# Issuing the window-cache copies of samples 0 to 3 during the output projection instead of the input projections

## The chip, the cores and the metric

The kernel runs on one core of one Trainium2 chip. The metric is device time in microseconds (us) of one execution. Times are given as the median of several executions; the profile shows one execution.

## The reference

One inference step of a one-layer decoder, for a prompt of 512 tokens and for 8 samples of 8 new tokens each (64 rows). Model width is 1024, all in 32-bit floats. Cut to what matters here:

```python
mod = (silu(c) @ w_ada + b_ada)                     # shift, scale and gate, 6 x 1024 per sequence
proj = (x * (1 + scale1) + shift1) @ w_in           # 1024 -> 3072: q, k, v of mixers A and B
oa, (wk, wv) = attend_a(qa, ka, va)                 # dilated window attention, 8 heads x 64
ob = rms_norm(attend_b(qb, kb, vb, lam), subln_g)   # differential attention, 4 heads
mixed = concatenate([oa, ob]) @ w_o
x = layer_norm(ALPHA * x + gate1 * mixed)
u = (x * (1 + scale2) + shift2) @ w_up + b_up       # 1024 -> 5632
uc = causal_conv3(u, w_conv) + b_conv
y = (gelu(uc[:half]) * uc[half:]) @ w_down + b_down
x = layer_norm(ALPHA * x + gate2 * y)

# for the samples, mixer A also returns its window buffers, moved on by the 8 new rows:
kk = concatenate([cache_win_k, k], 1)               # (8, 2048 + 8, 8, 64)
vv = concatenate([cache_win_v, v], 1)
return o, (kk[:, 8:], vv[:, 8:])                    # outputs win_k_sample, win_v_sample
```

The last line is what the change is about: of each sample's key window and value window, 2040 old rows of 2 KB each go unchanged from an input array to an output array. That is 4,080 KB (4.18 million bytes) per array and sample, 16 such copies in all.

## The kernel before, in words

Five engines run their own instruction lists and meet at semaphores: PE (matmul), DVE, ACT, POOL and SP. SP computes nothing; it waits and issues nearly all DMAs, on one queue (q1). ACT issues a part of the value-cache loads on a second one (q10).

The stages, in order of time in the profiled execution:

1. Up to about 58 us: constants, the conditioning vector, the first `w_ada` chunks, x transposed and modulated.
2. About 58 to 250 us: the input projection, six sections `s` of 512 columns, each for five row tiles `t` (four of the prompt, and `TP` = 4, the samples). Each section needs one 2 MB chunk of `w_in`. After a section, SP loads the next free chunk.
3. About 250 to 310 us: the prompt's attention A, with the other `w_ada` chunks loading; about 310 to 655 us: the samples' attention over their caches, with the prompt's attention B between.
4. About 690 to 756 us: the output projection, over the row tiles `WO_TILES = [0, 1, TP, 2, 3]`. DVE adds the residual and normalises each tile (L1355 is the last instruction of a tile and raises `x1_ok`). SP then stores the tile to the scratch array `spill` (L623), because `x_sb` is overwritten by the next stage: ACT's casts into `x_sb_r` (L806) wait for `spilled`.
5. About 771 to 1058 us: the up projection, 44 steps `k` of 128 columns. A `w_up` chunk (two DMAs of 1 MB, L470) holds four steps. Steps 0 to 3 read chunk up0, 4 to 7 up1, 8 to 11 up2, 12 to 15 up3, and so on. There are two buffers for raw chunks, so the load of up(i+2) is issued when PE has finished up(i) (`w_used`).
6. The down projection, the last norm, the stores.

Every weight is split into a high part and a rest before PE can use it. In the up projection, DVE makes the high part of a quarter of the chunk after next use (`high_of_piece(12 + k)`, a CAST at L1037) at the head of its step `k`, ahead of that step's convolution (L1411 to L1418); POOL then makes the rest (L741) at the head of its own step `k`. PE's step 4i waits for a quarter's rest before each quarter of its products (`wl_rest`). So the four quarters of up2 are made in steps 4 to 7 of DVE and POOL and are read from step 8 on.

The copies between input and output are made by one helper, which touches no engine but the DMA engines:

```python
def move_window(i, names=(("cache_win_k", "wks"), ("cache_win_v", "wvs"))):
    for name, dst in names:
        sp.dma_start(o[dst][0, i, 0:PAST - DS], a[name][0, i, DS:PAST]).then_inc(copied, 16)
```

`copied` is waited for only at the very end. Before the change, both copies of sample 0 are issued ahead of the projection sections, those of samples 1 to 3 after sections 0 to 2; the eight copies of samples 4 to 7 are issued one at a time behind the loads of up2 to up9.

Of the kernel before, what the change touches and what calls it, by code (L numbers as in the profile page):

```python
# [52 lines left out]
def chunk_before(n):  # L53

    return max((i for i in range(n) if SLOT_OF[i] == SLOT_OF[n]), default=None)
# [19 lines left out]
def build(nc, a, o, spill):  # L75
# [6 lines left out]
    with ctx:  # L82
# [3 lines left out]
        def sem(name):  # L86
            return ctx.enter_context(nc.semaphore(name))
# [40 lines left out]
        def slot(i, t=ring):  # L128
            return t[:, i * SLOT:(i + 1) * SLOT].rearrange("p (k n) -> p k n", k=KT_D)
# [120 lines left out]
        ada_ok = sem("ada_ready")  # L250
# [203 lines left out]
        def _(sp):  # L454
            def load_chunk(n):
                kind, i = CHUNKS[n]
                if (prev := chunk_before(n)) is not None and CHUNKS[prev][0] == "down":
                    half, kg = divmod(CHUNKS[prev][1], 3)
                    sp.wait_ge(g_used, FT * half + min(FT, 8 * kg + 8))
                elif prev is not None:  # L460
                    sp.wait_ge(w_used, prev + 1)
                if CHUNKS[n] == ("ada", 6):
                    sp.wait_ge(w_used, CHUNK_AT[("in", 5)] + 1)
                s = w_in_slot[SLOT_OF[n]]
                dst = slot(SLOT_OF[n])
                src = a[{"ada": "w_ada", "in": "w_in", "o": "w_o", "up": "w_up", "down": "w_down"}[kind]][0]
                src = src.rearrange("(k p) n -> p k n", p=P)
                if kind == "up":
                    for g in range(2):
                        sp.dma_start(dst[:, :, 256 * g:256 * g + 256],  # L470
                                     src[:, :, DFF * g + 256 * i:DFF * g + 256 * i + 256]).then_inc(s, 16)
                elif kind == "down":
                    half, kg = divmod(i, 3)
                    nk = min(8, FT - 8 * kg)
                    sp.dma_start(dst[:, 0:nk, :], src[:, 8 * kg:8 * kg + nk, CH * half:CH * half + CH]).then_inc(s, 16)
                else:
                    sp.dma_start(dst, src[:, :, CH * i:CH * i + CH]).then_inc(s, 16)
# [32 lines left out]
# [5 lines that stand above are left out]
            def flat(ap):  # L515
                return ap.rearrange("t h d -> t (h d)")

            sp.wait_ge(ada_ok, 4)
            move_window(0)
            n_rope = n_v = 0  # L520
            for n, (s, t) in enumerate(units):
                kb_rows = slice(P * t, P * t + P)
                if s in (0, 3):
                    n_rope += 1
                elif s in (1, 4):
                    m = s // 3
                    sp.wait_ge(rope_ok, n_rope + 1)
                    if t < TP:
                        st = n_rope % 4
                        dst = flat((o["wkp"] if m == 0 else o["kkp"])[0, 0])[kb_rows, :]  # L530
                        sp.dma_start(dst, stage[:, st, :]).then_inc(stg[st], 16)
                    else:
                        if m == 0:
                            for b in range(DB):
                                sp.dma_start(flat(o["wks"][0, b])[PAST - DS:PAST, :],
                                             k_s[DS * b:DS * b + DS, 0, :]).then_inc(out_sem, 16)
                        else:
                            sp.dma_start(o["kks"][0].rearrange("b s h d -> (b s) (h d)"), k_s[:, 1, :]).then_inc(out_sem, 16)
                    n_rope += 1
                else:  # L540
                    m = s // 3
                    n_v += 1
                    sp.wait_ge(pj_a, n_v)
                    if t < TP:
                        dst = flat((o["wvp"] if m == 0 else o["kvp"])[0, 0])[kb_rows, :]
                        sp.dma_start(dst, vp[:, t, m, :]).then_inc(out_sem, 16)
                    elif m == 0:
                        for b in range(DB):
                            sp.dma_start(flat(o["wvs"][0, b])[PAST - DS:PAST, :],
                                         v_s[DS * b:DS * b + DS, 0, :]).then_inc(out_sem, 16)  # L550
                    else:
                        sp.dma_start(o["kvs"][0].rearrange("b s h d -> (b s) (h d)"), v_s[:, 1, :]).then_inc(out_sem, 16)
                if t == TP:
                    load_chunk(6 + s)
                    if s < 3:
                        move_window(s + 1)
            for n in range(12, 18):
                load_chunk(n)

# [55 lines left out]
                sp.dma_start(ln1[:, i, :], a[name].to_broadcast([P, D])).then_inc(ln_in, 16)  # L615
            sp.dma_start(st_r, a["state_conv"][0].rearrange("b j f -> (b j) f")).then_inc(st_in, 16)

            for i, t in enumerate(WO_TILES):
                if i == TP:
                    load_chunk(FIRST_LATE + 2)  # L620
                sp.wait_ge(x1_ok, i + 1)
                rows = P if t < TP else NS
                sp.dma_start(spill[P * t:P * t + rows, :], x_sb[0:rows, t, :]).then_inc(spilled if i < TP else spilled_last, 16)  # L623
            load_chunk(FIRST_LATE + 3)
            sp.wait_ge(st_mm, 11)
            for i, name in enumerate(("b_down", "ln2_g", "ln2_b")):
                sp.dma_start(ln2[:, i, :], a[name].to_broadcast([P, D])).then_inc(ln2_in, 16)
# [38 lines left out]
        def _(pool):  # L666
# [21 lines left out]
            for _, what, r in sorted(jobs):  # L688
                if what == "split":
                    n = CHUNK_AT[("in", r)]  # L690
                    for k in range(0, KT_D, 2):
                        if r == 0:
                            pool.wait_ge(in0_high, k // 2 + 1)
                        else:
                            pool.wait_ge(win_high, 4 * (r - 1) + k // 2 + 1)
                        w = slot(SLOT_OF[n])[:, k, :]
                        high, rest = pair_of(n, k)
                        nc.gpsimd.tensor_tensor(rest, w, high.bitcast(F32), ALU.subtract).then_inc(win_pool, 1)
                    if r == 0:
                        rest_of_ht(0)  # L700
                    continue
                s, t = units[rope_units[r]]
                sample_k = s in (1, 4) and t == TP
                pool.wait_ge(pj_d, r + 1)
                if not sample_k and r >= 4:
                    if (prev := last_t[r]) is not None:
                        pool.wait_ge(qk_t, prev)
                    if (q := last_store[r]) > 0:
                        pool.wait_ge(stg[r % 4], 16 * q)
                rows = P if t < TP else NS  # L710
                dst = k_s[:, s // 3, :] if sample_k else stage[0:rows, r % 4, :]
                nc.gpsimd.tensor_tensor(dst, tmp_a[0:rows, r % 2, :], tmp_b[0:rows, r % 2, :], ALU.add)\
                    .then_inc(rope_ok, 1)
# [56 lines left out]
        def _(act):  # L770
# [47 lines left out]
            for _, what, n in sorted(jobs):  # L818
                s, t = units[n]
                rows = P if t < TP else NS  # L820
                if what == "v":
                    act.wait_ge(pj_mm, n + 1)
                    dst = vp[:, t, s // 3, :] if t < TP else v_s[:, s // 3, :]
                    nc.scalar.activation(dst, bk(n % 4)[0:rows, :], ACT.Copy).then_inc(pj_a, 1)
                else:
                    k = tr_units.index(n)
                    act.wait_ge(qk_t, k + 1)
                    src = bk(4 + k % 2).rearrange("p (f t) -> p f t", f=4)
                    m0 = 8 * (s // 3)
                    for h in range(2):  # L830
                        last = nc.scalar.activation(qtp[64 * h:64 * h + 64, m0 + h:m0 + 8:2, P * t:P * t + P],
                                                    src[64 * h:64 * h + 64], ACT.Copy)
                    last.then_inc(qk_a, 1)
# [1208 lines left out]
```

## Time and profile before

| | |
|---|---|
| median of 3 runs | 1250.76 us (1249.6 to 1254.75) |
| the profiled execution | 1249.29 us, of which the span from first to last instruction is 1247.3 us |
| mean granted PE clock | 0.911 of full speed |
| busy: PE, DVE, POOL, ACT | 1059.1, 838.5, 356.9, 269.2 us |
| queue q1 (SP) | 250.82 MB, 59.2% of 16 DMA engines' span |
| queue q10 (ACT) | 24.19 MB, 5.7% |
| the window copies | 16 of 4,080 KB |

The profile has a timeline of instructions for each engine. For a DMA it gives the time at which it was issued and how long the issuing engine was held, and separately the time from issue to landing, when its semaphore is raised. Busy shares are averages over stages with different limits; what one stage costs has to be read from its own windows.

### The profile page before, as it was taken

What the parts mean: (1) busy time and instruction counts of PE and PEld (TensorE: products, weight loads), DVE (VectorE), ACT (ScalarE), POOL (GpSimd) and SP (SyncE); (2) the same over time, 40 slices, a digit from 0 to 9 for tenths busy, and PEclk for the clock granted to TensorE, in tenths of its full rate; (3) what the DMA queues carried; (4) which work ended last, traced back from release to release, by engine and by line L of the source; (5) the groups of instructions that cost most, each with busy time, mean ns of one, the idle gap of its engine ahead of it and who ended that gap; (6) DMA issues with size and microseconds to landing.
All of it is one profiled execution on the core that took longest, in us unless ns stands there. A gap on an engine that the chain in (4) does not pass through costs nothing.

```text
span 1247.3 us, 24201 instructions
## 1 busy us (share of the span) xinstructions
PE 1059.1 (85%) x9389; PEld 856.2 (69%) x9389; DVE 838.5 (67%) x1521; ACT 269.2 (22%) x588; POOL 356.9 (29%) x378
## 2 busy tenths in 40 slices
PE   4599999999677677777776996999999999999994
PEld 2377777666455455555545774999999999777772
DVE  1657457267665767667749568367677676998968
ACT  0310010232222223222234103223222232100002
POOL 2333243100000000000007004356565565434323
PEclk8699999999787788779787897999999999999997
DMA  8948894686999999999991206177557731412202
GB/s 305 404 163 314 306 363 148 215 298 231 315 296 307 336 352 303 342 326 320 317 316 60 63 26 219 62 275 270 203 202 254 283 137 69 147 56 89 75 27 76
DMA packets 112551, 276.55 MB, mean 222 GB/s; under 512 B 9608, under 2 KB 33174, under 8 KB 108837
## 3 DMA queue, kind: packets, MB, share of 16 engines
q1 hardware_dynamic: 99125, 250.82, 59.2%
q10 hardware_dynamic: 13312, 24.19, 5.7%
q8 instruction: 75, 1.23, 0.4%
q14 instruction: 39, 0.32, 0.1%
HBM read 264.60 MB, written 76.69 MB: 274 GB/s over the span
## 4 chain that ended last, share of the span: by engine, by line
PE 58%; DVE 17%; SPq 10%; DMA 7%; issue 5%; POOL 2%; ACT 1%; ACTq 0%; DVEq 0%; POOLq 0%; PEldq 0%
PE wide L1572 16%; PE wide L1573 15%; PE wide L1574 15%; DVE ring L1145 3%; DMA ring<-in_cache_k 3%; SPq L591 3%; PE wide L1646 2%; SPq L593 2%; DMA ring<-in_w_ada 2%; PE wide L1635 2%; DVE ring_r L1077 2%; PE wide L1521 1%; SPq L448 1%; DMA ring<-in_w_down 1%; PE wide L1697 1%
## 5 line engine op out<-in xcount | busy, mean ns | idle before, releaser
L741 POOL TENSOR_TENSOR ring_r<-ring,ring_r 128x1024 fp32r<-128x1024 f32 x70 | 184.4, 2642 | 273.5 <-DVE ring_r L1037 204.5
L1572 PE MATMUL wide<-x_sb_r,ring_r 128*128 128x288 f32 x704 | 211.6, 301 | 8.2 <-DVE ht_r L1059 5.1
L1573 PE MATMUL wide<-ht_r,ring_r 128*128 128x288 f32 x704 | 209.4, 298 | 0.0
L1574 PE MATMUL wide<-x_sb_r,ring_r 128*128 128x288 f32 x704 | 208.6, 296 | 0.0
L1574 PE MATMUL wide<-ring_r,ht_r 128*128 128x512 f32 (+1 forms) x400 | 158.7, 397 | 0.0
L1145 DVE STREAM_TRANSPOSE ring<-ring 128x512 f32<-128x512 f32 x208 | 129.2, 674 | 34.7 <-DMA ring<-in_cache_k 34.7
L1572 PEld LDWEIGHTS wide<-x_sb_r,ring_r 128*128 128x128 f32 x704 | 133.4, 190 | 11.7 <-issue 11.2
L1574 PEld LDWEIGHTS wide<-x_sb_r,ring_r 128*128 128x128 f32 x704 | 134.2, 191 | 0.0
L1573 PEld LDWEIGHTS wide<-ht_r,ring_r 128*128 128x128 f32 x704 | 133.8, 190 | 0.0
L1697 PE MATMUL wide<-ring,x_sb 128*32 128x128 f32 (+1 forms) x1792 | 70.9, 309 | 49.5 <-DVE ring L1145 47.9
L1572 PE MATMUL wide<-ring_r,x_sb_r 128*128 128x512 f32 (+1 forms) x240 | 97.7, 407 | 11.0 <-DVE ht_r L1059 8.9
L1697 PEld LDWEIGHTS wide<-ring,x_sb 128*32 128x32 f32 x1792 | 54.5, 127 | 66.9 <-DVE ring L1145 57.5
L723 POOL COPY x_sb<-ring 32x128 f32<-32x128 f32 x64 | 18.4, 287 | 272.9 <-PE wide L1697 270.8
L1573 PE MATMUL wide<-ring_r,x_sb_r 128*128 128x512 f32 (+1 forms) x240 | 95.1, 396 | 0.0
L1572 PE MATMUL wide<-ring_r,ht_r 128*128 128x512 f32 (+1 forms) x220 | 88.2, 401 | 4.3 <-DVE ht_r L1397 2.4
L1574 PEld LDWEIGHTS wide<-ring_r,ht_r 128*128 128x128 f32 (+1 forms) x400 | 72.6, 181 | 21.5
L1573 PE MATMUL wide<-ring_r,ht_r 128*128 128x512 f32 (+1 forms) x220 | 86.7, 394 | 0.0
L1411 DVE SCALAR_TENSOR_TENSOR room<-room,vec_t 128x512 f32<-128x512 f32 x44 | 59.9, 1361 | 39.7 <-ACT room L954 39.6
L946 ACT ACTIVATE room<-wide,vec_t 128x576 f32<-128x576 f32 x44 | 32.7, 744 | 206.2 <-PE wide L1574 201.5
L1413 DVE SCALAR_TENSOR_TENSOR room<-room,vec_t 128x512 f32<-128x512 f32 x44 | 69.5, 1579 | 1.6
L1646 PE MATMUL wide<-room 128*128 128x128 f32 x320 | 58.3, 320 | 11.0 <-ACT room L866 9.8
L1037 DVE CAST ring_r<-ring 128x1024 fp32r<-128x1024 f32 x62 | 41.9, 687 | 36.1 <-DMA ring<-in_w_up 29.7
(225 smaller groups left out, 1894.0 us busy)
## 6 DMA issues: line engine op xcount, KB each, us to landing
ring<-in_cache_k SPq DMA_DIRECT2D x128, 256.0 KB
out_wks<-in_cache_win_k SPq DMA_DIRECT2D x8, 4080.0 KB, 19.0
out_wvs<-in_cache_win_v SPq DMA_DIRECT2D x8, 4080.0 KB, 24.7
ring<-in_w_ada SPq DMA_DIRECT2D x12, 2048.0 KB, 10.2
ring<-in_w_up SPq DMA_DIRECT2D x22, 1024.0 KB, 7.3
ring<-in_cache_win_k SPq DMA_DIRECT2D x16, 1024.0 KB
ring<-in_w_in SPq DMA_DIRECT2D x6, 2048.0 KB, 18.5
room<-in_cache_v ACTq DMA_DIRECT2D x32, 256.0 KB
```

The costliest lines, as they stand in the source:

```text
L591: pg = sp.value_load(pages[0:1, N_PAGES * b + 4 * g + t:N_PAGES * b + 4 * g + t + 1], min_val=0, max_val=a["cache_k"].shape[1] - 1)
L741: nc.gpsimd.tensor_tensor(rest, w, high.bitcast(F32), ALU.subtract).then_inc(wl_rest, 1)
L946: nc.scalar.activation(u_b[:, k % 2, 2:2 + NT].rearrange("p (h t) -> p h t", h=2), pair, ACT.Identity, bias=vec_t[:, 0, 48 + f:49 + f]).th ...
L1037: nc.vector.tensor_copy(pair_of(n, slice(k, k + 2))[0], slot(SLOT_OF[n])[:, k:k + 2, :]).then_inc(wl_high, 1)
L1145: last = nc.vector.transpose(ktg[:, G % NK, :, 32 * t:32 * t + 32], kraw[G % NK][:, t, :].rearrange("p (g d) -> p g d", d=32))
L1411: then(nc.vector.scalar_tensor_tensor(out=c_p, in0=u_b[:, k % 2, 1:1 + SEQ], scalar=tap(1), in1=c_p, op0=ALU.mult, op1=ALU.add))
L1413: nc.vector.scalar_tensor_tensor(out=c_p, in0=u_b[:, k % 2, 0:SEQ], scalar=tap(0), in1=c_p, op0=ALU.mult, op1=ALU.add)
L1572: nc.tensor.matmul(out, left[0], right[0], start=first, stop=False)
L1573: nc.tensor.matmul(out, left[0], right[1], start=False, stop=False)
L1574: return nc.tensor.matmul(out, left[1], right[0], start=False, stop=last)
L1646: last = nc.tensor.matmul(bank[:, 0:P], pt_b[:, u % 2, P * kb:P * kb + P], vp[:, kb, m, P * (n // 2):P * (n // 2) + P], start=(kb == 0), s ...
L1697: last = nc.tensor.matmul(bank[32 * nn:32 * nn + 32, at:at + nk], qbd[:, w % 2, g].rearrange("p i q -> p (i q)"), keys[:, g, 0:nk], start= ...
```

## The change

The four calls of `move_window` for samples 0 to 3 leave the projection stage. Samples 0 and 1 (four copies) are issued right after the loads that precede the output projection's tiles, samples 2 and 3 (four copies) right behind the load of chunk up1 (`FIRST_LATE + 3`). A wait of SP on `ada_ok` that stood ahead of the first call goes as well.

```diff
-            sp.wait_ge(ada_ok, 4)
-            move_window(0)
             n_rope = n_v = 0
             for n, (s, t) in enumerate(units):
...
                 if t == TP:
                     load_chunk(6 + s)
-                    if s < 3:
-                        move_window(s + 1)
             for n in range(12, 18):
                 load_chunk(n)
...
             sp.dma_start(st_r, a["state_conv"][0].rearrange("b j f -> (b j) f")).then_inc(st_in, 16)
 
+            move_window(0)
+            move_window(1)
             for i, t in enumerate(WO_TILES):
                 if i == TP:
                     load_chunk(FIRST_LATE + 2)
...
             load_chunk(FIRST_LATE + 3)
+            move_window(2)
+            move_window(3)
             sp.wait_ge(st_mm, 11)
```

Only SP's list changes. From the load of the gains and of the convolution state ahead of the output projection (`st_r`) to the load of up2, SP issues this before the change (each row is a DMA, destination and source, shape; L623 stores the tiles, the two L470 rows load up0 and up1):

```order
L616 DMA room<-in_state_conv 16x5632
L623 DMA x_spill<-x_sb 128x1024 x2
L623 DMA x_spill<-x_sb 64x1024
L623 DMA x_spill<-x_sb 128x1024
L470 DMA ring<-in_w_up 128x8x256 x2
L623 DMA x_spill<-x_sb 128x1024
L470 DMA ring<-in_w_up 128x8x256 x2
L627 DMA room<-in_b_down 128x1024
L627 DMA room<-in_ln_g 128x1024
L627 DMA room<-in_ln_b 128x1024
L470 DMA ring<-in_w_up 128x8x256 x2
```

In the changed kernel, the same stretch of SP's list, up to the load of the last gain row:

```order
L612 DMA room<-in_state_conv 16x5632
L512 DMA out_wks<-in_cache_win_k 64x16320
L512 DMA out_wvs<-in_cache_win_v 64x16320
L512 DMA out_wks<-in_cache_win_k 64x16320
L512 DMA out_wvs<-in_cache_win_v 64x16320
L621 DMA x_spill<-x_sb 128x1024 x2
L621 DMA x_spill<-x_sb 64x1024
L621 DMA x_spill<-x_sb 128x1024
L470 DMA ring<-in_w_up 128x8x256 x2
L621 DMA x_spill<-x_sb 128x1024
L470 DMA ring<-in_w_up 128x8x256 x2
```

```order
L512 DMA out_wks<-in_cache_win_k 64x16320
L512 DMA out_wvs<-in_cache_win_v 64x16320
L512 DMA out_wks<-in_cache_win_k 64x16320
L512 DMA out_wvs<-in_cache_win_v 64x16320
L627 DMA room<-in_b_down 128x1024
L627 DMA room<-in_ln_g 128x1024
L627 DMA room<-in_ln_b 128x1024
```

Four copies now stand ahead of the tile stores and the load of up0, and four more stand behind the load of up1, ahead of three row loads and the load of up2.

## Rows read from the trace of the kernel before

**Rows 1.** The page: busy time of each engine, its share, instructions
```profile
PE 1059.1 (85%) x9389; PEld 856.2 (69%) x9389; DVE 838.5 (67%) x1521; ACT 269.2 (22%) x588; POOL 356.9 (29%) x378
```

**Rows 2.** Stages: window, length; busy by engine; PE clock, DMA share, GB/s
```profile
58.00:250.00 192.00, 187.03 (x857) 141.06 (x858) 104.79 (x193) 19.80 (x40) 57.23 (x49) 0.99 0.74 256
704.00:750.00 46.00, 45.85 (x226) 33.61 (x225) 30.22 (x52) 0.81 (x4) 0.00 (x0) 1.00 0.09 29
780.00:803.00 23.00, 23.00 (x165) 23.00 (x165) 8.55 (x16) 6.80 (x8) 9.72 (x16) 0.94 0.00 1
```

**Rows 3.** Waits of PE, 58 to 250 us, the longest one
```profile
PE wide L1623 <- PE wide L1574: 1.8, 4, 0.5
```

**Rows 4.** Timeline of SP in the projections: issue time, SP held for
```profile
47.33 0.59 SPq L512 DMA_DIRECT2D out_wks<-in_cache_win_k  x1
47.97 0.94 SPq L512 DMA_DIRECT2D out_wvs<-in_cache_win_v  x1
...
151.19 0.41 SPq L477 DMA_DIRECT2D ring<-in_w_in  x1
151.64 10.88 SPq L512 DMA_DIRECT2D out_wks<-in_cache_win_k  x1
```

**Rows 5.** Landing of L512's copies issued from 40 to 60 us
```profile
DMA to landing us min/median/max: 18.3/24.1/29.8
```

**Rows 6.** Landing of L477's load issued at 151.19 us
```profile
DMA to landing us min/median/max: 19.8/19.8/19.8
```

**Rows 7.** Timeline of SP, output and up projection
```profile
693.73 0.43 SPq L616 DMA_DIRECT2D room<-in_state_conv  x1
714.28 36.76 SPq L623 DMA_DIRECT2D x_spill<-x_sb  x4
751.09 1.52 SPq L470 DMA_DIRECT2D ring<-in_w_up  x2
...
766.15 1.49 SPq L470 DMA_DIRECT2D ring<-in_w_up  x2
...
803.87 1.01 SPq L470 DMA_DIRECT2D ring<-in_w_up  x2
804.92 1.20 SPq L512 DMA_DIRECT2D out_wks<-in_cache_win_k  x1
830.00 1.00 SPq L470 DMA_DIRECT2D ring<-in_w_up  x2
```

**Rows 8.** Landing of L616's load, issued at 693.73 us
```profile
DMA to landing us min/median/max: 8.3/8.3/8.3
```

**Rows 9.** Landing of L470's two halves of up0, issued from 751.09 us
```profile
DMA to landing us min/median/max: 6.2/7.4/8.6
```

**Rows 10.** The same for up1: second half issued at 766.6 us
```profile
L470 SPq DMA_DIRECT2D ring<-in_w_up x2: 435/724/1012, 766.1 to 766.6; - x2
DMA to landing us min/median/max: 6.2/7.5/8.7
```

**Rows 11.** The same for up2: second half issued at 804.3 us
```profile
DMA to landing us min/median/max: 5.5/6.7/8.0
```

**Rows 12.** Landing of L512's copy issued at 804.92 us
```profile
DMA to landing us min/median/max: 18.7/18.7/18.7
```

**Rows 13.** Timeline of DVE: start, length, line, [idle before it, releaser]
```profile
762.37 3.37 DVE L1355 TENSOR_TENSOR x_sb<-x_sb,room 128x1024 f32<-128x1024 f32 x1
...
839.61 0.69 DVE L1037 CAST ring_r<-ring 128x1024 fp32r<-128x1024 f32 x1 [4.06 <-DMA ring<-in_w_up]
```

**Rows 14.** Timeline of POOL: rest of up3's last quarter
```profile
856.92 2.40 POOL L741 TENSOR_TENSOR ring_r<-ring,ring_r 128x1024 fp32r<-128x1024 f32 x1 [1.39 <-DVE ring_r L1037]
```

**Rows 15.** Timeline of ACT: first modulation of the second stage
```profile
766.52 2.78 ACT L791 ACTIVATE ht<-wide,mod_t 128x512 f32<-128x512 f32 x4 [2.40 <-PE wide L1546]
```

**Rows 16.** Stages around the start of the up projection, columns as above
```profile
770.00:776.70 6.70, 3.83 (x12) 2.94 (x12) 6.70 (x6) 3.97 (x8) 6.28 (x4) 0.50 1.07 373
776.70:782.60 5.90, 5.87 (x23) 5.68 (x24) 2.77 (x3) 0.00 (x0) 3.53 (x3) 0.50 0.29 112
```

## Prediction

> **What bounds the kernel now.** I read the page first, then the busy time by stages, the waits of PE in the stage that loses the copies, and last SP's timeline with the landing times of its transfers in the stages that receive them. PE is busy 1059.1 us, 85% of the span [rows 1], but that is an average; what counts is the two ends of the move.
>
> At the end that is relieved, PE is busy 187.03 of the 192 us from 58 to 250 us, at a clock of 0.99, with the DMA engines at 0.74 of their time [rows 2]. The longest group of waits of PE there is 1.8 us, on PE itself [rows 3], and none of the groups names a DMA. So this stage is bound by PE and the copies are already hidden in it. At the receiving end the DMA engines are nearly idle for a while: 0.09 of 704 to 750 us, and 0.00 of 780 to 803 us [rows 2]. The question is whether the moved transfers fit into these two holes, because what is issued behind them on SP's queue has to land on time.
>
> **How the queue behaves.** Two copies issued at 47.33 and 47.97 us [rows 4] landed after 18.3 and 29.8 us [rows 5], at 65.6 and 77.8 us. They are served one after the other, 12.1 us each, which is 4.18 MB at 345 GB/s. A load issued behind a copy waits for it: the one at 151.19 us took 19.8 us [rows 6], where up2's second half, on an empty queue, took 8.0 us [rows 11]. And the queue is full at some point: SP was held for 10.88 us on the copy issued at 151.64 us [rows 4], when one earlier copy and the load were outstanding. So a third copy in a row will probably hold SP until the first has landed. That does not change the order or the rate, since the DMA engines keep work throughout.
>
> **What is removed.** Eight copies, 8 x 12.1 = 97 us of DMA time, out of the projections. No wait of PE hangs on them, so I take 0. The upper bound of a gain is all of PE's idle time in that stage, 192 - 187.03 = 5.0 us. The wait on `ada_ok` had nothing behind it but these copies and much later stores: 0.
>
> **What is added ahead of the tile stores (samples 0 and 1).** The load ahead of them lands at 693.73 + 8.3 = 702.0 us [rows 7, 8]. Four copies take 4 x 12.1 = 48.4 us and end at 750.4 us. Queued behind are the stores of tiles, the first of them ready at 714.28 us [rows 7]: three of 1.31 MB together, at 345 GB/s 3.8 us, to 754.2 us; the fourth (0.52 MB, issued just before 751.09 us) to 755.7 us; then up0, 2.10 MB, 6.1 us more, to 761.8 us. It landed at 751.6 + 8.6 = 760.2 us before [rows 7, 9], so it is 1.6 us late. ACT casts it, and ACT's next instruction behind those casts started at 766.52 us after 2.40 us of idleness that PE ended [rows 15]. That idleness covers the 1.6 us: 0. If the copies went at 13 us each, up0 would be 5.2 us late and some 3 us of it would reach PE; this is the upper bound. Below nothing, POOL's work on up0 would start later and no longer overlap the DVE instruction at 762.37 us, which took 3.37 us there [rows 13] and for which PE waits; I allow 2 us of gain. The stores themselves are needed by ACT's casts from 769 us on, well behind 755.7 us.
>
> **What is added behind up1 (samples 2 and 3).** This is the term that decides.
> - up1 lands at 766.6 + 8.7 = 775.3 us [rows 10]. Four copies: + 48.4 = 823.7 us. The hole from 780 to 803 us takes only about half of them.
> - Behind them come three row loads of 0.52 MB and up2 of 2.10 MB, together 3.67 MB. At the 373 GB/s that loads reached from 770 to 776.7 us [rows 16] that is 9.8 us. up2 is there at 833.5 us; before, its second half landed at 804.3 + 8.0 = 812.3 us [rows 11].
> - From landing to use: in up3, where DVE and POOL did the same four steps with almost no wait for PE, the first cast started at 839.61 us on the load's landing [rows 13] and the last quarter's rest was ready at 856.92 + 2.40 = 859.3 us [rows 14], so 19.7 us. For up2 the last quarter would be ready at 833.5 + 19.7 = 853.2 us.
> - PE uses it at three quarters of step 8. Steps take (830.00 - 803.87) / 4 = 6.5 us [rows 7], step 8 begins at 830.0 us, so the need is at 834.9 us. PE stops for 853.2 - 834.9 = 18.3 us, in four pieces within step 8. Put otherwise: up2 could land as late as 815.2 us without harm, 2.9 us later than before, and it lands 21 us later.
> - The clock: after a stretch with PE half idle (3.83 of 6.70 us busy), it was granted 0.50 and kept that for another 5.9 us of continuous work [rows 16]. The same after this stall costs 0.5 x 5.9 = 3.0 us. Bounds 0 and 4 us.
> - Later chunks: up3 is issued at 830.0 us as before, lands behind sample 4's copy (12.1 us) at about 851 us, and DVE comes to it only after step 7, at about 855 us. PE's step 12 has moved by 21 us as well, and up4 is issued 21 us later into an idle queue. So the delay is paid once. The other direction: were up3 more than about 4 us later still, each us would be added.
>
> Queued behind SP's held issues are only DMAs of this same list, and nobody but PE, through DVE and POOL, waits for them at that time.
>
> **The rate.** For a copy alone I have 12.1 us from the pair; the copy issued at 804.92 us landed after 18.7 us [rows 7, 12], 11.3 us after up2 (812.3 us). With 11.3 us each up2 would land 3.2 us earlier, so the stall would be 15 us. I take 12.1 us, since it is the one taken between two copies in a row, which is what happens here.
>
> The Trainium skill says in "DMA: Bandwidth & Descriptors", section "Anatomy of one DMA", that a transfer costs some 2.0 us plus its bytes at 436 GB/s (a fit for DMAs issued by GpSimd). By it a copy in a row would take 9.6 us, the four 38.4 us, the stall would be 8.3 us, and the estimate of the whole change +11 us instead of +21. The trace disagrees for this kind of copy, which reads and writes main memory: 12.1 us.
>
> **Sum.** 0 + 0 + 18.3 + 3.0 = +21.3 us. The profiled execution took 1249.3 us, so 1270.6 us. It lies 1.5 us under the median of the runs, so I predict a median of 1271 to 1272 us, say 1271.5.
>
> **The rivals.**
> 1. *The first four copies bite too* (12 in 100). If they take 13 us each, or if SP, held on the third and fourth copy, is late with the stores, the stage at 770 us starts 3 to 5 us late on top. For it: the margin is only about 2 us. Against: ACT's idleness [rows 15], and a queue that should be empty of copies at 750 us. Time: 1275 to 1278 us.
> 2. *Half the stall* (10 in 100). Copies are faster when fewer other transfers run, or DVE and POOL catch up faster than 19.7 us. A rate near that of loads, 373 GB/s, gives 11.2 us for each copy and a stall of 14.7 us; a catch-up at DVE's bare busy time would take a few us more off. Time: 1258 to 1266 us. The skill's rule above is at this end too.
> 3. *The copies are not in the way* (6 in 100). If later loads overtook earlier copies on the queue, up2 would be on time and nothing else changes: 1250 us. The 19.8 us against 8.0 us speak against it.
> 4. *Faster* (4 in 100). One mechanism: without copies beside them the projections lose their idle time, 5.0 us, and some of the matmuls' own slack. It decides only if up2 lands by 815.2 us, which needs rival 3's overtaking too, or copies of under 7.5 us each. For it: DMA share of 0.74 in that stage. Against: no wait there names a DMA. Time: 1243 to 1246 us.
>
> **How the numbers follow.** The forecast (68 in 100) spans its own bounds: stall 15 to 20, clock 0 to 4, early gain 0 to 5, output projection -2 to +3, mostly not all at one end: +14 to +25 us, 1264 to 1275 us on the median. With rival 1 above and the upper part of rival 2 below, 1260 to 1278 us holds about 8 in 10. What a measurement of this kernel can tell from no change is about 0.5%, 6.3 us: faster 0.04, same 0.06, slower 0.90.
>
> **What would show it.** In the changed kernel's profile: (a) PE's busy time and clock from 58 to 250 us as before, and every stage up to 690 us at the same time within 2 us; (b) DMA share near 1 from 702 to 750 us and from 775 to 833 us; (c) SP held for about 12 us on the third and the fourth copy of each group; (d) up2's landing 27 to 30 us after its issue, and DVE's first wait at L1037 for `in_w_up` grown from 4 to about 25 us; (e) PE waiting at L1572 for POOL's L741 at step 8, some 18 us in all, with the clock at 0.50 in and after it; (f) steps of 6.5 us again from step 9 on. The prediction is wrong if PE's stage up to 250 us gets shorter by more than 2 us, or if a second chunk is late.

## The result, and the profile after

The changed kernel takes 1270.4 us (median of 4 runs, 1267.25 to 1271.24) against 1250.18 us before (median of 4, 1245.33 to 1254.75). The ratio is 1.0156, with a 95% interval of 1.0133 to 1.0179: slower by 20 us. The forecast was 1271.5 us.

The page after: the span and the busy times.

```profile
span 1265.3 us, 24201 instructions
PE 1060.6 (84%) x9389; PEld 857.1 (68%) x9389; DVE 833.2 (66%) x1521; ACT 269.7 (21%) x588; POOL 352.6 (28%) x378
```

The span is 18.0 us longer. PE is busy only 1.5 us longer than in [rows 1]; the other 16.5 us are idleness of PE. The windows of the changed kernel (columns as in [rows 2]) say where:

```profile
58.00:250.00 192.00, 187.11 (x874) 140.59 (x877) 106.46 (x200) 20.35 (x41) 57.30 (x49) 1.00 0.29 101
702.00:750.00 48.00, 47.85 (x236) 35.29 (x235) 30.55 (x52) 0.81 (x4) 0.00 (x0) 1.00 0.97 330
775.00:833.00 58.00, 52.78 (x372) 52.37 (x372) 14.38 (x26) 12.23 (x15) 12.69 (x21) 0.94 0.99 334
830.00:860.00 30.00, 15.45 (x78) 14.59 (x79) 23.40 (x26) 6.08 (x8) 18.63 (x25) 0.77 1.00 368
```

The projections lost 60% of their DMA work (0.74 to 0.29) and PE is as busy there as before: 187.11 against 187.03 us. The output projection now has the DMA engines full, 0.97 against 0.09, and PE does not notice. Of these windows, the one in which PE is half idle is that from 830 us on. SP's timeline there (issue time, SP held for):

```profile
713.94 36.77 SPq L621 DMA_DIRECT2D x_spill<-x_sb  x4
750.75 1.73 SPq L470 DMA_DIRECT2D ring<-in_w_up  x2
...
763.66 1.52 SPq L470 DMA_DIRECT2D ring<-in_w_up  x2
765.22 1.61 SPq L512 DMA_DIRECT2D out_wks<-in_cache_win_k  x1
...
768.14 0.59 SPq L512 DMA_DIRECT2D out_wvs<-in_cache_win_v  x1
...
803.42 20.12 SPq L470 DMA_DIRECT2D ring<-in_w_up  x2
823.58 3.49 SPq L512 DMA_DIRECT2D out_wks<-in_cache_win_k  x1
829.55 0.99 SPq L470 DMA_DIRECT2D ring<-in_w_up  x2
...
875.50 0.99 SPq L470 DMA_DIRECT2D ring<-in_w_up  x2
```

The last two rows are the loads of up3 and up4, issued at the starts of PE's steps 8 and 12. Between them lie 45.95 us. Steps 4 to 7 took 26.13 us in [rows 7], and so did steps 8 to 11 of the kernel before, where up3 was issued at 830.00 us and up4 here:

```profile
856.14 1.00 SPq L470 DMA_DIRECT2D ring<-in_w_up  x2
```

So 19.8 us are lost in this one place. The queue was busy with the copies behind up1. The landings of the first of them, then of the third and the fourth, then of the last two row loads, then of up2's halves:

```profile
DMA to landing us min/median/max: 20.2/20.2/20.2
DMA to landing us min/median/max: 42.2/48.4/54.7
DMA to landing us min/median/max: 56.2/56.7/57.2
DMA to landing us min/median/max: 26.7/27.9/29.1
```

With the issue times that is 765.22 + 20.2 = 785.4 us and 768.14 + 54.7 = 822.8 us, so 12.5 us per copy; 769.88 + 57.2 = 827.1 us; 803.8 + 29.1 = 832.9 us. DVE, PE and POOL then show what follows (start, length, [idle before, releaser]):

```profile
832.92 0.69 DVE L1037 CAST ring_r<-ring 128x1024 fp32r<-128x1024 f32 x1 [24.99 <-DMA ring<-in_w_up]
```

```profile
836.62 0.58 PE L1572 MATMUL wide<-x_sb_r,ring_r 128*128 128x288 f32 x1 [7.19 <-POOL ring_r L741]
841.67 0.40 PE L1572 MATMUL wide<-x_sb_r,ring_r 128*128 128x288 f32 x1 [1.84 <-POOL ring_r L741]
847.68 0.61 PE L1572 MATMUL wide<-x_sb_r,ring_r 128*128 128x288 f32 x1 [4.15 <-POOL ring_r L741]
852.83 0.40 PE L1572 MATMUL wide<-x_sb_r,ring_r 128*128 128x288 f32 x1 [1.94 <-POOL ring_r L741]
```

```profile
850.05 2.72 POOL L741 TENSOR_TENSOR ring_r<-ring,ring_r 128x1024 fp32r<-128x1024 f32 x1 [1.39 <-DVE ring_r L1037]
```

The reader is to see the chain: a load that lands 20.6 us later than in [rows 11], one quarter after another made by DVE and POOL at their own pace, and PE waiting for POOL four times, 15.1 us in all, in step 8. No wait names the copies; they are two steps back.

### The profile page after: what moved, and what is told of

Same layout as the page of the kernel before. It is cut to its first block, busy times and chain, and to the rows that moved or that the text cites. A ratio compares the mean times of both kernels' runs of the same rounds, so it can differ in the third digit from the quotient of the medians.

```text
span 1265.3 us, 24201 instructions
## 1 busy us (share of the span) xinstructions
PE 1060.6 (84%) x9389; PEld 857.1 (68%) x9389; DVE 833.2 (66%) x1521; ACT 269.7 (21%) x588; POOL 352.6 (28%) x378
## 3 DMA queue, kind: packets, MB, share of 16 engines
q8 instruction: 75, 1.23, 0.4%
## 4 chain that ended last, share of the span: by engine, by line
PE 53%; DVE 16%; SPq 12%; DMA 9%; issue 5%; POOL 3%; ACT 1%; ACTq 0%; DVEq 0%; POOLq 0%; PEldq 0%
PE wide L1572 15%; PE wide L1574 14%; PE wide L1573 14%; SPq L587 3%; SPq L589 3%; DVE ring L1145 3%; DMA ring<-in_cache_k 3%; DMA ring<-in_w_up 2%; PE wide L1646 2%; DMA ring<-in_w_ada 2%; PE wide L1635 2%; DVE ring_r L1077 2%; SPq L448 2%; POOL ring_r L741 1%; PE wide L1521 1%
## 5 line engine op out<-in xcount | busy, mean ns | idle before, releaser
L1572 PE MATMUL wide<-x_sb_r,ring_r 128*128 128x288 f32 x704 | 213.6, 303 | 25.5 <-POOL ring_r L741 15.1
L1572 PEld LDWEIGHTS wide<-x_sb_r,ring_r 128*128 128x128 f32 x704 | 135.4, 192 | 29.3 <-issue 20.5
L1574 PEld LDWEIGHTS wide<-x_sb_r,ring_r 128*128 128x128 f32 x704 | 136.1, 193 | 0.0
L1411 DVE SCALAR_TENSOR_TENSOR room<-room,vec_t 128x512 f32<-128x512 f32 x44 | 54.4, 1236 | 46.3 <-ACT room L954 46.3
L1413 DVE SCALAR_TENSOR_TENSOR room<-room,vec_t 128x512 f32<-128x512 f32 x44 | 71.3, 1619 | 1.6
## 6 DMA issues: line engine op xcount, KB each, us to landing
ring<-in_w_ada SPq DMA_DIRECT2D x12, 2048.0 KB, 10.3
```

What stands on the lines that cost most here:

```text
L1411: then(nc.vector.scalar_tensor_tensor(out=c_p, in0=u_b[:, k % 2, 1:1 + SEQ], scalar=tap(1), in1=c_p, op0=ALU.mult, op1=ALU.add))
L1413: nc.vector.scalar_tensor_tensor(out=c_p, in0=u_b[:, k % 2, 0:SEQ], scalar=tap(0), in1=c_p, op0=ALU.mult, op1=ALU.add)
L1572: nc.tensor.matmul(out, left[0], right[0], start=first, stop=False)
L1574: return nc.tensor.matmul(out, left[1], right[0], start=False, stop=last)
```

## The experiments

Each was timed in five rounds beside the kernel before on the same chip, if not said otherwise; "us" behind a ratio is the ratio less one, times the median of before in the same session (1250.27, 1249.77 or 1251.91 us).

**Which half of the move costs.** Only the first pair of samples moved:

```diff
+                    if s in (1, 2):
+                        move_window(s + 1)
...
+            move_window(0)
+            move_window(1)
             for i, t in enumerate(WO_TILES):
```

> Only the four copies of samples 0 and 1 move, to just ahead of the output projection's tile stores; those of samples 2 and 3 stay in the projections. Theory A (all of the loss is the backlog behind up1): 0 us, -2 to +2, against the kernel before; up0 lands 1 to 2 us late, and up2 lands on time. Theory B (the first four copies bite as well, through up0 and the tile stores): +3 to +5 us. Theory C (the relief of the projections is worth its 5 us of idle time, and the loss behind up1 is larger than it looks): half of the relief shows alone here, -2 to -3 us.

Measured: 0.9994 (0.998 to 1.0008), -1 us. Only the second pair moved:

```diff
             load_chunk(FIRST_LATE + 3)
+            move_window(2)
+            move_window(3)
```

> Only the four copies of samples 2 and 3 move, to behind the load of chunk up1; those of samples 0 and 1 stay in the projections. Theory A: the whole loss, +18 to +21 us, with PE's four waits for POOL at step 8 of 15 us together and the clock at half in and after them. Theory B: +15 to +17 us. Theory C: +21 to +24 us.

Measured: 1.0167 (1.0149 to 1.0186), +21 us. The whole loss is here; theory B (the first four copies bite) is out. Against the changed kernel the stall itself is 3 us longer, in one execution of each. SP's timeline and DVE's first wait in this kernel:

```profile
765.73 1.52 SPq L470 DMA_DIRECT2D ring<-in_w_up  x2
...
829.44 3.06 SPq L470 DMA_DIRECT2D ring<-in_w_up  x2
878.57 0.99 SPq L470 DMA_DIRECT2D ring<-in_w_up  x2
```

```profile
835.03 0.69 DVE L1039 CAST ring_r<-ring 128x1024 fp32r<-128x1024 f32 x1 [27.20 <-DMA ring<-in_w_up]
```

Steps 8 to 11 take 49.13 us. up1, and the copies behind it, start 63.7 us ahead of step 8 here and 65.9 us ahead of it in the changed kernel. These 2 us come from the start of the up projection (below, under the first four copies).

**What the relief of the projections is worth.** The kernel before without the copies of samples 0 to 3, which leaves these rows of two outputs unwritten, and the same without any of the 16 copies:

```diff
-            sp.wait_ge(ada_ok, 4)
-            move_window(0)
...
-                    if s < 3:
-                        move_window(s + 1)
```

> The kernel before without the copies of samples 0 to 3: this leaves out half of the copies of the old window rows, so that these parts of two outputs stay unwritten. It prices the relief of the projections by itself. Theory A: 0 us, within 2 us, the projection stage as long as before, although 33.4 million bytes less go through the queue. Theory C: -3 to -5 us, with PE's idle time from 58 to 250 us gone.

Measured: 1.0001 (0.9986 to 1.0016), 0 us; PE is busy 187.07 of the 192 us from 58 to 250 us. Theory C is out.

> The kernel before without any of its 16 copies between input and output, so that the old window rows of two outputs stay unwritten. It prices all the copies in their old places. If they are hidden where they are: 0 us, within 2 us. If those of samples 4 to 7 cost anything where they stand behind up2 to up9, where DVE waits about 4 us for each of these loads, it shows as a gain of a few us here.

Measured: 1.001 (0.9989 to 1.0031), +1 us, within the noise. As far as these runs can tell, all 16 copies were free where they stood.

**Is there a threshold?** Two copies behind up1, then three, the others in the projections:

```diff
             load_chunk(FIRST_LATE + 3)
+            move_window(2)
+            move_window(3, (("cache_win_k", "wks"),))   # only in the run with three
```

> Only sample 2's two copies stand behind up1, all others where they were. Theory A gives a threshold: with 12.5 us per copy they end at 775 + 25 = 800 us, the three row loads at 804 us, up2 lands at 812 us or less than 1 us later, ahead of the 815.2 us at which it would begin to cost. So 0 us, within 2 us. A theory in which each copy behind up1 costs its share would have half of the loss, +9 to +10 us.

> Sample 2's two copies and sample 3's key copy stand behind up1, the other copies as before the change. By the threshold: copies end at 775.3 + 3 x 12.5 = 812.8 us, row loads at 817.1 us, up2 lands at 822.9 us, 7.7 us behind the last harmless time of 815.2 us; with some loss of clock +8 to +11 us. By equal shares: three quarters of the loss, +14 to +15 us.

Measured: two copies 0.998 (0.9963 to 0.9997), -2.5 us and under what can be told from no change; three copies 1.0076 (1.0052 to 1.01), +9.5 us. Equal shares would have given +10 and +15. There is a threshold: two copies cost nothing, the third about 10 us, the fourth another 10.

**Which bytes ahead of up2 count.** The changed kernel with the three row loads behind up2:

```diff
-            sp.wait_ge(st_mm, 11)
-            for i, name in enumerate(("b_down", "ln2_g", "ln2_b")):
-                sp.dma_start(ln2[:, i, :], a[name].to_broadcast([P, D])).then_inc(ln2_in, 16)
             for n in range(FIRST_LATE + 4, FIRST_LATE + 13):
                 load_chunk(n)
+                if n == FIRST_LATE + 4:
+                    sp.wait_ge(st_mm, 11)
+                    ...
```

> The changed kernel, with the three row loads (b_down and the two rows of the last norm, 1.57 million bytes) issued behind the load of up2 instead of ahead of it. They took 4.3 us of the queue in the changed kernel. If the queue's order and bytes set the stall, it shrinks by 4.3 us, so +15 to +16 us against the kernel before instead of +19 to +20. If it is SP's being held (20.12 us on up2's issue, until the last copy landed) that makes up2 late, up2 is issued at the same time and, with the load's own 8 us behind it, nothing or at most 1 us is gained.

Measured: 1.0131 (1.0091 to 1.0171), +16 us. The trace is the sharper view: SP was held for 8.60 us on up2 instead of 20.12, steps 8 to 11 took 42.41 us instead of 45.95, 3.5 us less (4.3 expected), and the first cast came 3.6 us earlier against the start of step 8. So the bytes ahead in the queue set the landing here. SP's being held did not: SP came free of up2 at 810.1 us, and up2's second half landed at 801.9 + 25.4 = 827.3 us, 6.0 us behind the last copy (821.3 us). The hold itself was not shorter, only divided: behind up2, SP was held for another 11.39 us on the first row load.

**Does another queue help?** The four copies of samples 2 and 3 issued by ACT:

```diff
-            move_window(2)
-            move_window(3)
...
+            for i in (2, 3):
+                for name, dst in (("cache_win_k", "wks"), ("cache_win_v", "wvs")):
+                    act.dma_start(o[dst][0, i, 0:PAST - DS], a[name][0, i, DS:PAST]).then_inc(copied, 16)
             act.wait_ge(halo, 1)
```

> The changed kernel, with the four copies of samples 2 and 3 issued by ACT on the second queue, at the same place in time (after ACT's casts for the first step, about 772 us), instead of by SP. If the loss comes from standing ahead of up2 in one queue, up2 shares the DMA engines with the backlog instead of waiting for all of it: its 3.7 million bytes with the rows at half the rate take about 12 to 16 us, landing at about 818 us, and the loss falls to 2 to 6 us. If all traffic is served in order of issue whatever the queue, the loss stays at 18 to 20 us. If ACT is held on its third and fourth copy, step 0's bank is emptied late and some 10 us are added at 785 us instead.

Measured: 1.0156 (1.0121 to 1.0191), +19.5 us. Nothing is gained. SP's timeline in this kernel:

```profile
765.63 1.61 SPq L625 DMA_DIRECT2D room<-in_b_down  x1
767.29 0.43 SPq L625 DMA_DIRECT2D room<-in_ln_g  x1
767.76 0.43 SPq L625 DMA_DIRECT2D room<-in_ln_b  x1
803.91 18.89 SPq L470 DMA_DIRECT2D ring<-in_w_up  x2
822.84 4.51 SPq L512 DMA_DIRECT2D out_wks<-in_cache_win_k  x1
...
873.93 0.99 SPq L470 DMA_DIRECT2D ring<-in_w_up  x2
```

The landings of ACT's last two copies, issued at 769.7 and 770.3 us, then of the first row load, of the other two, and of up2's halves, issued at 803.9 and 804.3 us:

```profile
DMA to landing us min/median/max: 43.8/49.7/55.6
DMA to landing us min/median/max: 26.3/26.3/26.3
DMA to landing us min/median/max: 48.2/53.7/59.3
DMA to landing us min/median/max: 25.6/27.1/28.5
```

The row loads went out before the first copy and on the other queue, and yet took 26 to 59 us, where they took 9 us in the kernel before: they landed at 791.9, 815.5 and 827.1 us, in between the copies at 787.7, 799.1, 813.5 and 825.9 us. So the two queues did share the DMA engines, but not by halves, as I had expected: between the landing of up1 (773.0 us) and 827.1 us, what landed from SP's queue were the 1.6 million bytes of the rows, and from ACT's the 16.7 million of the copies. up2 stood behind two of these row loads. Its first half was issued at 803.9 us without being held, and landed at 829.5 us, 2.4 us behind the last row load. SP was held on the second half, until 822.8 us; it landed at 832.8 us. ACT was not held on its issues (0.61 to 0.66 us each). Which of the two keeps up2 back here, the row loads ahead of it or the small share of its queue, no run separates; one with the row loads behind up2 and the copies on ACT's queue would.

**What holds SP.** Each of the four copies cut into two DMAs, a single run:

```diff
-            move_window(2)
-            move_window(3)
+            for i in (2, 3):
+                for name, dst in (("cache_win_k", "wks"), ("cache_win_v", "wvs")):
+                    for r in (0, 1020):
+                        sp.dma_start(o[dst][0, i, r:r + 1020], a[name][0, i, DS + r:DS + r + 1020]).then_inc(copied, 16)
```

> The changed kernel, with each of the four copies behind up1 issued as two DMAs of half its rows: the same bytes in eight DMAs. Time: +18 to +20 us as before the split, if queue bytes set the stall. It also asks what holds SP on the issue of up2. If a number of outstanding DMAs is the limit (9 with up2's first half in the changed kernel), SP is held already on the last of the copies or on the rows, at about 770 us. If it is their size in rows or bytes, SP is held only on up2, for about 20 us again.

Measured: 1266.29 us, +14 us against the median before, and less than expected. The stall is as long as expected all the same: steps 8 to 11 lost 20.2 us, but this execution had reached step 8 at 826.73 us, 3.3 us earlier than the profiled one of the kernel before. Eight copies and three rows were issued without being held, and SP was held for 19.99 us on up2 as before. A number of outstanding DMAs is not the limit. Nor are their bytes: in the changed kernel SP issued the last row load at 769.88 us without being held, with all four copies outstanding, and was held on up2 at 803.8 us, when the first two of them had landed (785.4 and 796.8 us). The number of pieces into which the DMAs are cut may be the limit, which stays open.

**Is it the burst or the traffic?** The same 16.7 million bytes in 32 pieces, one in each step of ACT:

```diff
+                if k < 32:
+                    i, r = 2 + k // 16, 255 * (k % 8)
+                    name, dst = (("cache_win_k", "wks"), ("cache_win_v", "wvs"))[(k // 8) % 2]
+                    act.dma_start(o[dst][0, i, r:r + 255], a[name][0, i, DS + r:DS + r + 255]).then_inc(copied, 16)
```

> The changed kernel, with the four copies of samples 2 and 3 cut into 32 pieces of 0.52 million bytes, one issued by ACT in each of the steps 0 to 31 of the up projection. The same bytes go through the same DMA engines in the same stage, but no backlog stands ahead of a load of a chunk: per chunk of four steps 2.1 + 4.18 + 2.1 = 8.4 million bytes, 24 us of 26 us at 345 GB/s. If the burst ahead of up2 is the cause, the loss falls to 0 to +4 us (the loads land 2 to 6 us later than before, against 3 us of room). If it is the added traffic in this stage itself, or the move out of the projections, the loss stays near 20 us.

Measured: 0.9998 (0.9975 to 1.0021), 0 us. The windows of this kernel over the up projection, and DVE's waits for chunks (us in total, times, longest):

```profile
804.00:1012.00 208.00, 205.54 (x1530) 203.89 (x1529) 151.90 (x172) 61.66 (x80) 118.06 (x156) 1.00 0.89 315
```

```profile
DVE ring_r L1039 <- DMA ring<-in_w_up: 31.2, 9, 5.0
```

The DMA engines are at 0.89 in this stage, the longest wait of DVE for a chunk is 5.0 us, and PE is busy all the time. The stage can carry these bytes; it can't carry them ahead of up2. The run with ACT's queue above issues the same bytes on the same queue in one burst: +19.5 us there, 0 us here.

**Lateness and loss.** Lateness is the start of the first cast of up2 less the last harmless time for it. That lies 14.8 us ahead of the start of step 8: the last quarter is used 4.9 us into the step, and takes 19.7 us to be made. The loss is the time from up3's to up4's issue less 26.13 us.

| kernel | first cast, us | step 8, us | lateness | loss in steps 8 to 11 |
|---|---|---|---|---|
| before | 812.30 | 830.00 | -2.9 | 0 |
| spread over ACT's steps | 815.57 | 832.18 | -1.8 | 0.0 |
| two copies | 809.93 | 828.00 | -3.3 | 0.0 |
| three copies | 820.75 | 827.13 | 8.4 | 10.3 |
| rows after up2 | 827.37 | 827.65 | 14.5 | 16.3 |
| on ACT's queue | 832.84 | 830.05 | 17.6 | 17.8 |
| half copies | 830.02 | 826.73 | 18.1 | 20.2 |
| changed kernel | 832.92 | 829.55 | 18.2 | 19.8 |
| second pair only | 835.03 | 829.44 | 20.4 | 23.0 |

The loss is the lateness plus 0.2 to 2.6 us where up2 is late, and nothing where it is not. Between a lateness of -1.8 and 8.4 us no run lies, so the threshold is not placed more closely than that.

## Why the prediction was right, point by point

- *The relief is worth 0*: right. 187.11 us of PE work in 192 us, and 0 us when the copies were dropped altogether.
- *The first four copies are hidden*: right, measured -1 us. They took 12.5 us each and not 12.1. up0's second half landed at 751.2 + 9.8 = 761.0 us, 0.8 us late instead of 1.6. The 2 us of gain that I had allowed did appear and did not last. DVE's L1355, 3.37 us in [rows 13], took 1.23 us, nearly all of it ahead of POOL's work on up0 (763.19 us), and up1's load was issued at 763.66 instead of 766.15 us. But step 4 began at 803.42 instead of 803.87 us, and the same 0.4 us had already been there at 692 us. In between PE waited 7.6 instead of 5.1 us for DVE's `ht_r`, with DVE's next work (L1386) at 2.25 instead of 1.21 us beside POOL's. What stayed is that the four late copies started 2.2 us earlier against step 8. This is not owed to the moved pair alone: the same instruction took 1.2 us in every run with the pair moved, but also in those with two copies behind up1 and with no copies, where the pair had not moved.
- *The four copies behind up1*: right in mechanism and nearly in every part. Landing of up2 832.9 us, forecast 833.5: the copies were 0.4 us slower each and began 2.5 us earlier. That these two misses nearly cancel is luck. From first cast to the last rest 852.77 - 832.92 = 19.85 us, forecast 19.7. The last quarter was late by 852.77 - 834.45 = 18.3 us, as forecast. PE's waits within the step add up to 15.1 us and not to 18, because a part of its products between them ran at half the clock.
- *The clock*: too large. 19.8 us were lost and 18.3 are lateness, so 1.5 us instead of 3.0. The mean over 830 to 860 us was 0.77, not 0.50, because PE went back and forth between half and full speed, as the lengths of its products show:

```profile
838.91 0.44 PE L1572 MATMUL wide<-x_sb_r,ring_r 128*128 128x288 f32 x1
842.97 0.29 PE L1572 MATMUL wide<-x_sb_r,ring_r 128*128 128x288 f32 x1
856.02 0.44 PE L1574 MATMUL wide<-x_sb_r,ring_r 128*128 128x288 f32 x1
```

  A product takes 0.44 us up to 839.8 us, 0.29 us from 841.9 to 843.5 us, 0.45 us from 847.7 to 850.9 us, and, behind the last wait, 0.44 us from 854.1 to 857.5 us only. These 3.4 us at half speed cost 1.7 us by estimate, where 5.9 us had been assumed.
- *The delay is paid once*: right. From up4 on, the loads follow at 26.1 us (875.50, 901.64, 927.77 us), and up2's is the only wait of DVE that grew, to 25 us.
- *SP is held on the third and fourth copy*: wrong. It issued the copies in 0.6 to 1.6 us each, and was held for 20.12 us on up2's load instead. This changed no term of the sum, because the queue still had rows to serve until 827.1 us when SP came free at 823.5 us. The reading of [rows 4] had left something out: SP had issued eight stores of 16 KB (L549, 148.48 us) just ahead of the load at 151.19 us, so more may have been outstanding than one copy and the load.
- *The page on DMA*: its fit of 2.0 us plus bytes at 436 GB/s ("DMA: Bandwidth & Descriptors", section "Anatomy of one DMA", in the Trainium skill) would make +11 us by estimate; the copies took 12.5 us each in a row, and the loss was 20 us. The trace does not agree for copies from main memory to main memory.

From the end of the stall to the end of the kernel 1.5 us came back: the first part of the down projection ran at a clock of 1.00, where the kernel before had 0.78 from 1066 to 1072 us. In the kernel with the second pair only, it did not come back. I take it for chance of the clock; no run was made to show it.

## What to carry to other kernels

A transfer that nobody waits for is free only while the gap in front of the next transfer that somebody does wait for is longer than it. Add up what the queue must serve between two such loads and compare it with that load's last harmless time, here 15 us ahead of the step that uses it, because of the two engines that prepare it. A large copy is better cut into pieces that fit between the loads than issued at once, and an idle stretch of DMA time is no reason to move work out of a stage where it was already hidden.

## What was not expected of the hardware

- SP can be held for long on an issue, and neither the number nor the bytes of the outstanding DMAs tell when. It was held for 20.12 us on up2 with two copies left, and not at all 34 us earlier with four. Cutting the copies into twice as many DMAs changed nothing (19.99 us), and taking the three row loads out from between only divided the hold (8.60 us on up2, 11.39 us on the first row load).
- The other queue is no way around a burst. With 16.7 million bytes of copies on ACT's queue, row loads of 0.52 million bytes on SP's queue took 26 to 59 us instead of 9, and SP was held on up2 for 18.89 us, while ACT had been held on none of its four copies. Whether the copies held SP themselves, or through the two row loads that they kept from landing, is not shown.
- Copies from main memory to main memory took 12.5 us for 4.18 million bytes in a row, 334 GB/s counted once, both ahead of the output projection's tiles and behind up1 (12.1 us at 47 to 78 us in the kernel before).
